# A backbone kernel on one Trainium2 core: modulation weights in smaller pieces through four buffers, the first norm's statistics in the prologue, and the second layer's modulation inside the first projection

## What is computed

```python
s_lat, s_ctx = silu(c), silu(c_ctx)
for i in range(2):                                   # ada_w[i]: (1024, 6144), 24 MB a layer
    m_lat = split(s_lat @ ada_w[i] + ada_b[i], 6)    # shift, scale, gate, shift, scale, gate
    m_ctx = split(s_ctx @ ada_w[i] + ada_b[i], 6)
    h = rmsnorm(x, norm1_g[i]) * (1.0 + m[1]) + m[0]
    x = x + m[2] * mixer_i(h)                        # layer 0 begins with u = h @ ev_w_in
    x = x + m[5] * swiglu(rmsnorm(x, norm2_g[i]) * (1.0 + m[4]) + m[3])
```

## Time and profile before

| | us |
|---|---|
| median of 3 runs (lowest, highest) | 3553.22 (3545.87, 3558.02) |
| the profiled execution: its time, its span | 3556.72, 3555.1 |
| PE busy over the span | 3253.5 (92%) |
| PEld, DVE, ACT, POOL busy | 2512.4, 1560.7, 952.2, 357.5 |
| prologue, from the start to the first instruction of `even_in` | 268.3 |

### The profile page before, as it was taken

How to read it: one execution, slowest core, us unless ns; L and a number is a source line. 1 busy time by engine, 2 the same in 40 slices (tenths; PEclk the granted TensorE clock), 3 DMA queues, 4 the chain that set the end, 5 groups by cost and what they waited for, 6 DMA issues and landing times. The chain is left out here.

```text
span 3555.1 us, 37659 instructions
## 1 busy us (share of the span) xinstructions
PE 3253.5 (92%) x15050; PEld 2512.4 (71%) x15050; DVE 1560.7 (44%) x1826; ACT 952.2 (27%) x1085; POOL 357.5 (10%) x252
## 2 busy tenths in 40 slices
PE   5878998799965799999999999899987899999999
PEld 2337885455554678888888888777766788888887
DVE  5305315666678533333223322567665432342333
ACT  2124112344411213111111111376773311111111
POOL 3000000077721110000000000200001000000000
PEclk8878999799987999999999999899998999999999
DMA  6772210000211411111111111201102111111112
GB/s 244 276 276 88 85 50 3 0 1 1 115 56 42 154 35 30 36 37 40 39 36 36 42 37 36 80 30 38 35 30 104 51 53 48 47 47 47 47 47 77
DMA packets 45560, 228.95 MB, mean 64 GB/s; under 512 B 6376, under 2 KB 6760, under 8 KB 39178
## 3 DMA queue, kind: packets, MB, share of 16 engines
q1 hardware_dynamic: 41594, 203.37, 16.6%
q10 hardware_dynamic: 1728, 13.63, 0.9%
q0 software_dynamic: 2128, 10.36, 0.7%
HBM read 201.65 MB, written 25.69 MB: 64 GB/s over the span
## 5 line engine op out<-in xcount | busy, mean ns | idle before, releaser
L252 PE MATMUL bank<-h_hi,w_hi 128*128 128x512 f32 (+1 forms) x2616 | 704.5, 369 | 15.3 <-DVE h_lo L1645 7.2
L252 PE MATMUL bank<-h_lo,w_hi 128*128 128x512 f32 (+1 forms) x2616 | 701.3, 368 | 0.0
L252 PE MATMUL bank<-h_hi,w_lo 128*128 128x512 f32 (+1 forms) x2616 | 700.7, 368 | 0.0
L238 DVE TENSOR_TENSOR w_lo<-w_raw,w_hi 128x1024 fp32r<-128x1024 f32 x194 | 262.6, 1354 | 662.8 <-ACT w_hi L232 658.0
L252 PEld LDWEIGHTS bank<-h_hi,w_hi 128*128 128x128 f32 x2616 | 452.9, 188 | 100.4 <-issue 15.7
L252 PEld LDWEIGHTS bank<-h_lo,w_hi 128*128 128x128 f32 x2616 | 453.0, 188 | 88.4 <-issue 3.1
L252 PEld LDWEIGHTS bank<-h_hi,w_lo 128*128 128x128 f32 x2616 | 452.7, 188 | 85.3
L1577 DVE SCALAR_TENSOR_TENSOR x<-bank,c_mods,x 128x1024 f32<-128x1024 f32 (+3 forms) x280 | 271.8, 1006 | 254.9 <-PE bank L252 254.8
L232 ACT ACTIVATE w_hi<-w_raw 128x1024 fp32r<-128x1024 f32 x194 | 203.8, 1051 | 647.2 <-PE bank L252 610.5
L252 PE MATMUL bank<-hid_hi,w_hi 128*128 128x512 f32 (+1 forms) x880 | 242.3, 373 | 11.6 <-DVE x L1577 11.6
L252 PE MATMUL bank<-hid_lo,w_hi 128*128 128x512 f32 (+1 forms) x880 | 240.1, 370 | 0.0
(11 more groups left out here) (284 smaller groups left out, 3673.3 us busy)
## 6 DMA issues: line engine op xcount, KB each, us to landing
w_raw<-in_weights SPq DMA_DIRECT2D x194, 512.0 KB, 3.5
ada_w<-in_ada_w SPq DMA_DIRECT2D x32, 1536.0 KB, 7.7
x<-in_x SPq DMA_DIRECT2D x2, 5120.0 KB, 18.6
h_gate<-u_scratch SPq DMA_DIRECT2D x4, 2560.0 KB, 9.3
u_scratch<-uc POOLq DMA_DIRECT2D x12, 640.0 KB, 3.2
spec_lat<-f_spec ACTq DMA_DIRECT2D x2, 3584.0 KB, 10.3
h_spec<-spec_lat SPq DMA_DIRECT2D x2, 3584.0 KB, 12.5
x_kept<-x SPq DMA_DIRECT2D x1, 4096.0 KB, 13.0
```

Source lines behind the costliest of these rows:

```text
L238: e.tensor_tensor(k.w_lo[s][:, :], k.w[s][:, :], k.w_hi[s][:, :].bitcast(F32), ALU.subtract).then_inc(k.split_lo[s], 1)
L252: mm = e.matmul(out[:, c:c + m], w[:, c1:c1 + P], x[:, c:c + m], start=(first and kk == 0 and n == 0), stop=(last and kk == kt - 1 and n = ...
```

## The change

- `Stream`: a load is two column tiles (1 MB, 48 loads) where it was three. The first 24 loads, layer 0, go through four buffers in the prologue: 10 ahead of order 0's transforms, 4 ahead of order 1's, and one after each of groups 2 to 6 of each "lat". PE turns load n-1 after it has multiplied load n.
- The last 24 loads, layer 1, are made in `even_in`: one after item 0 and two after item 1 of each of the 8 pairs behind the first, in PSUM banks 6 and 7. They have one buffer, `late_w`: SP issues load n when the products of load n-1 are done, and these waits stand in SP's queue between the loads of the projection's weights.
- The statistics of the first norm (`Norm.tensor`, `invert`, `root`) move from `even_in` to the prologue, between the two orders; the taps of order 1 wait for them, as they use the same banks. Coefficients of norm 0 are made there, those of norms 1 to 3 at the end of DVE's part of `even_in`.
- The transform table is loaded ahead of `x`, some small tiles are placed elsewhere, and loops of the two blocks are unrolled.

```diff
-ADA_M = 3
+ADA_M = 2
 ADA_LOADS = 2 * 48 // ADA_M
+ADA_BUFS = 4
+ADA_FIRST = 2 * KT // ADA_M
+ADA_EARLY = ADA_LOADS // 2
...
     def load(self, k, e):
+        for n in range(ADA_EARLY):
+            if n >= ADA_BUFS:
+                e.wait_ge(self.sums, n - ADA_BUFS + 1)
+            e.dma_start(self.w[n % ADA_BUFS][:, :, :], k.d["ada_w"][n]).then_inc(self.full[n % ADA_BUFS], 16)
+
+    def load_late(self, k, e, n):
+        if n > ADA_EARLY:
+            e.wait_ge(self.sums, n)
+        e.dma_start(self.late_w[:, :, :], k.d["ada_w"][n]).then_inc(self.late_full, 16)
...
+        for n in range(self.made, self.made + count):
+            w, group = self.w[n % ADA_BUFS] if n < ADA_EARLY else self.late_w, self.group(n)
+            if n < ADA_EARLY:
+                e.wait_ge(self.full[n % ADA_BUFS], 16 * (n // ADA_BUFS) + 16)
+            else:
+                e.wait_ge(self.late_full, 16 * (n - ADA_EARLY) + 16)
+            if n >= 2:
+                e.wait_ge(self.stored, n - 1)
...
+            mm.then_inc(self.sums, 1)
+            if n and n != ADA_EARLY:
+                self.turn(k, e, n - 1)
...
@@ prologue
+    ADA_AT = (10, 4)
...
+            e.dma_start(tab[:, :], d["tab_f"]).then_inc(tab_landed, 16)
             e.dma_start(k.x[:, :, :], d["x"]).then_inc(x_landed, 16)
-            e.dma_start(tab[:, :], d["tab_f"]).then_inc(tab_landed, 16)
...
+                    if g == NT:
+                        e.wait_ge(k.rr_ready, len(norm.chunks))
...
-                ada.products(k, e, 4)
+                ada.products(k, e, ADA_AT[order])
...
-                        if part == "lat" and pos in (2, 4):
+                        if part == "lat" and pos >= 2:
                             ada.products(k, e, 1)
-            ada.products(k, e, ADA_LOADS // 2 - ada.made)
+                if order == 0:
+                    e.wait_ge(hw_ready, NT)
+                    norm.tensor(k, e)
+            ada.products(k, e, ADA_EARLY - ada.made)
+            ada.turn(k, e, ADA_EARLY - 1)
...
+                if j == 1:
+                    norm.root(k, e)
...
@@ even_in
-            load_weights(k, e, ph)
+            late = ADA_EARLY
+            for i in range(ph.pairs):
+                load_next(k, e, i + w0)
+                if i:
+                    for n in range(3):
+                        k.ada.load_late(k, e, late)
+                        late += 1
...
-            with e.Fori(0, ph.pairs - 1) as i:
+            for i in range(ph.pairs - 1):
                 for s in range(2):
                     item(k, e, s, i + (w0 + 1), i + (a0 + 1), k.rhs_h, T)
+                    k.ada.products(k, e, 1 + s)
+            k.ada.turn(k, e, ADA_LOADS - 1)
...
             fold_gains(k, e)
+            e.wait_ge(k.ada.stored, ADA_LOADS)
+            k.ada.gate_bias(k, e, coef_steps)
+            k.ada.coefficients(k, e, coef_steps, [1, 2, 3])
```

More of the change, by code:

```diff
@@ L372, in __init__ @@
         words = KT * ADA_M * P
[L373 to L383, removed]
+        places = (S0, S0 + words, END - 2 * words, END - words)
+        assert 2 * words <= 4 * WS and H0 + 29056 <= END - 2 * words
@@ new lines, in __init__ @@
+        self.w = [k.at(f"ada_w{n}", at, [P, KT, ADA_M * P]) for n, at in enumerate(places)]
+        self.full = [k.sem(f"ada_landed{n}") for n in range(ADA_BUFS)]
+        late = R0 + 10240
+        assert late + words + 2 * ADA_M * P <= END and ADA_EARLY % ADA_BUFS == 0
+        self.late_w, self.late_full = k.at("ada_late_w", late, [P, KT, ADA_M * P]), k.sem("ada_late_landed")
+        late_row = [k.at(f"ada_late_row{s}", late + words + s * ADA_M * P, [P, ADA_M * P]) for s in range(2)]
+        self.sums, self.read, self.stored, self.columns = (k.sem(f"ada_{n}") for n in ("sums", "read", "stored", "columns"))
@@ L386, in load @@
     def load(self, k, e):
[L387 to L392, removed]
-    def products(self, k, e, count):
[L396 to L412, removed]
@@ new lines, in load, with turn @@
+        for n in range(ADA_EARLY):
[6 more added lines that the diff above has]
+        e.dma_start(self.late_w[:, :, :], k.d["ada_w"][n]).then_inc(self.late_full, 16)
+    def turn(self, k, e, n):
+        e.wait_ge(self.read, n + 1)
+        for m in range(ADA_M):
+            tr = e.matmul(self.turned(n)[:, 2 * m:2 * m + 2], self.row(n)[:, m * P:(m + 1) * P],
+                          k.c["pick"][:, :], start=True, stop=True)
+        tr.then_inc(self.columns, 1)
@@ L413, in products, with store @@
         self.made += count
+    def store(self, k, e, n):
+        e.wait_ge(self.columns, n + 1)
+        e.activation(k.mods[:, 2 * ADA_M * n:2 * ADA_M * (n + 1)], self.turned(n), ACT.Copy).then_inc(self.stored, 1)
     def copy(self, k, e, count):
[L417 to L425, removed]
+        for n in range(self.copied, self.copied + count):
+            e.wait_ge(self.sums, n + 1)
+            if n >= 2:
+                e.wait_ge(self.columns, n - 1)
+            e.activation(self.row(n)[:, :], self.out(n), ACT.Copy).then_inc(self.read, 1)
+            if n and n != ADA_EARLY:
+                self.store(k, e, n - 1)
@@ L706, in _ @@
                 if part == "lat":
-                    ada.copy(k, e, 4)
+                    ada.copy(k, e, ADA_AT[order])
                 if j:
@@ L773, in centres @@
                              bias=k.hy_b[:, bass.ds(i * 2 + s, 1)]).then_inc(centre, 1)
-            with e.Fori(0, HP) as i:
+            for i in range(HP):
                 for s in range(2):
```

75 lines of the change are left out of this document (54 added, 21 removed).

## The result

The changed kernel takes 3621.22 us (median of 4 runs, 3610.58 to 3624.51) against 3551.67 for the kernel before in the same comparison: ratio 1.0184 [1.0168, 1.0200]. The medians lie 69.5 us apart; by the ratio it is 65. I had forecast 3589 and a range up to 3604. The direction and most of the steps held; the time lies outside the range. The profiled execution took 3620.53 with a span of 3618.9, which is 63.8 above the span before.

What follows compares the result with a forecast made beforehand. PE was taken to bound the projection (busy 21.50 of 21.50 us, full clock), while prologue PE time was cheap. Terms -44.2 - 6.3 + 35.0 + 35.2 + 14.4 + 2.3 = +36.4 on 3553.2 gave 3589 us, range 3563 to 3604.

Steps and rivals of the forecast that it cites:

- (a): Start of the prologue: ten loads at 3.0 us each, ending at 88 where it was 97.42.
- (b): Prologue, order 0's "lat" transforms: 28.5 us with five single-load insertions, so DVE's L495 comes at 116.5.
- (c): Between the orders: norm's root waits behind ACT's 9.95 us store wait; order 1's taps start at 136.1 against 135.87.
- (d): Prologue, order 1: taps take the long 17.43 us, until 153.6; transforms start at 174.3 instead of 182.32.
- (e) and (f): Prologue's end: `even_in` starts at 224.1, 44.2 us earlier; there the first `xr` skips the statistics, 6.3 us more.
- (g): Projection: 24 late products and turns on a PE without free time, 1.46 us each, add 35.0 us.
- (j): Projection's end: one more turn and store, 14 coefficient steps on DVE, less ACT's last copy; adds 2.3 us.
- (h): Projection, after item 1: PE waits 4.4 us for the single late buffer in each of 8 pairs, 35.2 us.
- (i): Projection: low PE clock behind each of the 8 stalls loses 1.8 us, 14.4 us; bounds 0 and 8 x 2.2.
- the longer landing: Projection: second late load lands in 6.2 us (3601) or 7.7 (3613); chance 0.16, shared with less prologue gain.
- the clock that holds: Projection gaps cost no clock and order 1's taps take 9.61 us; time 3567; chance 0.2, in part or whole.
- The late load that isn't waited for: PE's second product after item 1 waits nothing, so the change is faster: 3540 us; chance 0.04.

Runs made afterwards that it cites:

- e4: Changed kernel with the first norm's statistics back at the head of the projection (`even_in`); 3612.58 us, ratio 1.0166 to the kernel before.
- e1: Changed kernel with the late weights loaded only once, all 24 late products reading that load (wrong weights); 3577.69 us, ratio 1.0076 to before.
- e3: Changed kernel with 24 throwaway matmuls keeping PE busy in each of the 8 gaps; 3589.76 us, ratio 1.0103 to before.
- e6: Changed kernel with 16 late loads, one behind each item, 32 in the prologue, and norm statistics back in the projection; 3551.27 us, ratio 0.9989 to before.
- e5: Changed kernel with 16 late loads instead of 24, one behind each item, and 32 in the prologue; 3562.81 us, ratio 1.0026 to before.
- e7: Changed kernel with 24 late loads spaced inside the items and norm statistics back in the projection; 3546.27 us, ratio 0.9973 to before.
- e2: Changed kernel, same 24 late loads, products spaced: inside item 0, inside item 1, behind item 1; 3559.62 us, ratio 1.0008 to before.
- e8: Changed kernel with all 48 loads in the prologue through four buffers, norm statistics back in the projection; 3574.10 us, ratio 1.0047 to before.

## Why the prediction was off, point by point

- (a) The ten products ended at 84, not 88: the first six came faster, four of them with 1.07 each. The later ones, at the low clock, came every 3.23 (against 3.0).
- (b) Right in its end, partly by luck: the "ctx" transforms, which wait for the step that I put at 116.5, began at 115.83. The "lat" transforms started 4 early but took 31.6 instead of 28.5, since their first records still ran at the low clock (1.91 to 2.06 for two, against 1.02).
- (c) Mis-sized: I took the 9.95 of before for ACT's wait for the spectrum's store, and it was 14.69. The taps started at 139.58, not at 136.1. It isn't the statistics, for e4 has 14.37 without them. It is the load issued just ahead of the store, as the windows above show: before had none in flight. All eight experiments have such a load there and wait 14.1 to 14.7; the store after order 1 took 9.73 in each of those in which the loads were through by then.
- (d) Right for this execution, but not certain: the taps took 17.40 (17.43), and transforms of order 1 started 3.5 late, as (c) left them. In e1 and e3, with the same prologue, they took 9.65.
- (e) and (f) Right in sum: the last store's issue was 1.4 late, its wait 9.73, the block ended at 224.48 (forecast 224.1), and the first product came at 234.07. What I did not see is that the move of the norm, which I booked as 6.3 gained, costs (c) and (d) more than it gains: e4 gives 6 to 9 us for taking it back, e6 against e5 11.5, and e7 against e2 12.4 by the ratios.
- (g) Nearly right: 24 x 1.46 = 35.0. With (j), 37.3 were forecast; e2 has 40.3 for the two, and after 39.6 when its stalls and its clock are taken off the 100.6.
- (h) Right: 8 waits, 35.1 us in all (forecast 35.2). The Trainium skill (DMA: Bandwidth & Descriptors, Bandwidth) would have made it 47; the trace did not agree, with 4.8 at the median for 1 MB.
- **(i) is the step of the sum that failed, by its size.** I read the length of the low clock off the gap at 314 and took 3.6 us at half speed, 1.8 lost. Here it lasts 7.4, and 3.5 are lost, against my upper bound of 2.2: seven times 3.5 and 1.6 behind the last gap make 25.9 in the block, where I had 14.4. The gap that I read was 2.96 us and a full item followed it. Here it is 4.4, and a product of 256 columns and a turn follow before the item. Which of the two doubled the length was not tried apart. But the one row was too thin a basis anyhow. The gap at the same place of pair 1 is 3.0 us in every version, and the 10 us behind it had a mean clock of 0.83 before, 1.00 in after, and 0.70 in e1:

```profile
317.00:327.00 10.00, 9.99 (x43) 8.41 (x44) 4.67 (x5) 0.00 (x0) 1.09 (x2) 0.83 0.50 185
267.50:277.50 10.00, 9.92 (x51) 8.45 (x52) 4.67 (x5) 0.00 (x0) 1.08 (x2) 1.00 0.73 264
260.80:270.80 10.00, 9.99 (x37) 8.36 (x38) 4.67 (x5) 0.00 (x0) 1.08 (x2) 0.70 0.80 289
```

  The prediction's other gap, of 2.0 us ahead of the last "ctx" transforms, did cost no clock; its twin ahead of order 0's, 2.03 us as well, was followed by records of 1.91 against 1.02. The Trainium skill (TensorE: Matmul & The Clock Gate, HAM oscillation) has this pattern right, that every burst behind a DMA wait begins at the low clock; the trace agrees for all eight waits of 4.4, with 0.50 behind the gap and 0.88 over the pair, while behind a DMA wait of 1.71 in e3 the product took 1.07, at the full clock.
- (j) Nearly right to the start of `latents`, but what comes next was left out: PE has stood 3.73 instead of 1.57 there and begins that block at the low clock, and 12 records of L967 take 5.95, where the same of before take 4.11. Of the 3.3 lost 1.8 are these, the rest of what the eighth gap cost in clock. Another 1.4 are low clock behind PE's next wait, which ends at 618.46.
- **The sum put everything behind the projection at nothing, without a reason given, and that failed too.** The stages there came out 12.6 longer: the 3.3 of (j), 4.8 in Hyena, 4.2 in the SwiGLU stretch, 0.3 elsewhere. Hyena is 2 us above before in e1, e2, e7 and e8 and 5 above in e3 to e6; the SwiGLU stretch is within what the versions show among themselves (960 to 974). By the windows above, much of both is the clock of PE. Why it differs in stages with the same instructions stays open.
- The range's upper end, 3604, follows from no line: the longer landing gives 3601 at 6.2 us and 3613 at 7.7.

The account: forecast +36.4; (i) +11.5; (g) and (j) +2.3; (h) -0.1; the start 1.1 less early; the stretches behind the projection +12.6; that is 63.8, the difference of the spans, and 5.7 come from the executions compared. With (i) alone put right the forecast would have been 3601, inside the range; it took what came behind the projection as well to leave it.

Of the rivals, the clock that holds was wrong for the stalls, each of which cost clock; its other half, the taps at full clock, didn't come in after but did in e1 and e3. The longer landing was wrong (4.8). The late load that isn't waited for is what e2 built. It gave no change where I had put it 13 faster: 3 us in the projection, 3.3 at the start of `latents` and 9 in the SwiGLU stretch stand against it.

## What to carry to other kernels

Where one buffer serves a stream that is consumed inside a busy PE, spread the consumers so that each load has more than its landing time. Here three products per pair at 9 us or more apart cost nothing but themselves, and two side by side cost 63 us over eight pairs. A gap on PE is to be priced with the clock behind it, and from more than one gap: 4.4 us of gap cost 8 in all here, eight times alike, while gaps of 3.0 us at one place cost nothing in one version and 2.7 us in another. Before moving a step into an earlier block, look at what its queues hold there: the norm's root stood behind a store of 14.7 us on ACT, and that store behind a load. And where spans of single executions are compared, stages that the edit doesn't touch are to be compared too: here they differed by 12 us between after and e3.

## What the runs showed of the hardware

- The thin products didn't bring the clock back where it was low, and kept it where it was high. In e8 those of 256 columns stayed at 0.50 for 20 us, with PE busy in 17.88 of them (the window above). In e1 four of them, straight behind the taps at full clock, take 1.07 each. In the prologue of after three take 1.07 each, a wait for a load of 1.05 comes, one more takes 1.07, then a wait of 0.86, and from there each takes 1.93 up to 83.
- A short gap costs the clock in one place and not in the next: in e1 two of eight gaps of up to 1.41 us did, and its four runs spread over 27 us with the mean clock. Gaps of 3.0 us at one place of the program were followed by full clock in after and e2, and by a mean of 0.83 and 0.70 over 10 us in before and in e1.
- ACT's store of 3.5 MB took 14.7 us with a load of 1 MB from SP issued half a us ahead of it (15.4 in e5, with 1.9 MB beside it), and 9.7 alone in the same execution; before, alone too, it took 9.95. In after its first packet starts 4.4 us behind the issue at 115.39, when the load's packets are nearly through, and 0.8 us behind the issue where it is alone.
- Filling a wait of 4.4 us on PE with 24 throwaway matmuls of 248 columns kept the full clock behind it, and was worth 3.5 us a gap (e3).
